# Rotated rows of queries and keys fetched by transfers instead of rotation products

## The reference, cut to what matters

```python
q = apply_partial_rope(rms_norm_2(q.reshape(B, S, 2, DIFF_HEADS, HEAD_DIM), a_q_norm[l]), cos, sin)
k = apply_partial_rope(rms_norm_2(k.reshape(B, S, 2, DIFF_HEADS, HEAD_DIM), a_k_norm[l]), cos, sin)
...
o = diff_attention(q, k, v, lam).transpose(0, 2, 1, 3)
```

## Time and profile before

| | us |
|---|---|
| median of 3 runs | 2271.78 (2271.11 to 2274.24) |
| the profiled execution | 2271.08 |
| its span in the trace | 2269.3 |
| TensorE busy | 2147.4 (95% of the span) |
| VectorE busy | 1237.1 (55%) |
| ScalarE busy | 917.2 (40%) |
| differential stage, from its first to its last instruction | about 1676.6 to 1856 |

### The profile page before, as it was taken

How to read it: one execution, slowest core, us unless ns; L and a number is a source line. 1 busy time by engine, 2 the same in 40 slices (tenths; PEclk the granted TensorE clock), 3 DMA queues, 4 the chain that set the end, 5 groups by cost and what they waited for, 6 DMA issues and landing times. The chain is left out here.

```text
span 2269.3 us, 35754 instructions
## 1 busy us (share of the span) xinstructions
PE 2147.4 (95%) x14668; PEld 1577.5 (70%) x14668; DVE 1237.1 (55%) x2123; ACT 917.2 (40%) x1655; POOL 45.6 (2%) x36
## 2 busy tenths in 40 slices
PE   7999999899999899999989999998999988999998
PEld 5785654588888676766447888886877566887546
DVE  5555443766662375464447666424538774444554
ACT  5424434433332354154344333324346563424462
POOL 2000001000000020000010000000000000000000
PEclk9999999999999999999999999999999999999999
DMA  5201111122223221020112222222321102222001
GB/s 201 75 3 57 57 39 38 67 101 93 93 98 107 75 75 56 22 77 25 50 38 75 93 97 107 93 75 97 114 77 54 38 29 84 93 93 90 23 1 38
DMA packets 23922, 159.82 MB, mean 70 GB/s; under 512 B 3024, under 2 KB 3664, under 8 KB 4944
## 3 DMA queue, kind: packets, MB, share of 16 engines
q1 hardware_dynamic: 23760, 157.53, 19.5%
HBM read 155.43 MB, written 2.10 MB: 69 GB/s over the span
## 5 line engine op out<-in xcount | busy, mean ns | idle before, releaser
L675 DVE TENSOR_TENSOR arena_r<-ring,arena_r 128x512 fp32r<-128x512 f32 x480 | 333.0, 705 | 456.0 <-ACT arena_r L666 453.2
L666 ACT ACTIVATE arena_r<-ring 128x512 fp32r<-128x512 f32 x480 | 296.3, 629 | 601.2 <-PE banks L716 569.1
L714 PE MATMUL banks<-oT_r,arena_r 128*128 128x512 f32 x1136 | 463.0, 408 | 13.4 <-DVE arena_r L675 9.0
L716 PE MATMUL banks<-oT_r,arena_r 128*128 128x512 f32 x1136 | 445.4, 392 | 0.0
L715 PE MATMUL banks<-hT_r,arena_r 128*128 128x512 f32 x1008 | 394.7, 392 | 0.0
L714 PE MATMUL banks<-arena_r,arena_r 128*128 128x512 f32 x688 | 283.2, 412 | 18.0 <-DVE arena_r L706 10.7
L715 PE MATMUL banks<-arena_r,arena_r 128*128 128x512 f32 x720 | 283.2, 393 | 0.0
L716 PE MATMUL banks<-arena_r,arena_r 128*128 128x512 f32 x688 | 270.5, 393 | 0.0
L714 PEld LDWEIGHTS banks<-oT_r,arena_r 128*128 128x128 f32 x1136 | 215.0, 189 | 72.1 <-DVE arena_r L952 10.4
L716 PEld LDWEIGHTS banks<-oT_r,arena_r 128*128 128x128 f32 x1136 | 214.8, 189 | 45.7
L715 PEld LDWEIGHTS banks<-hT_r,arena_r 128*128 128x128 f32 x1008 | 190.5, 189 | 44.8 <-issue 7.9
(11 more groups left out here) (394 smaller groups left out, 2929.8 us busy)
## 6 DMA issues: line engine op xcount, KB each, us to landing
ring<-weights SPq DMA_DIRECT2D x142, 1024.0 KB, 4.8
xT<-x_features SPq DMA_DIRECT2D x2, 1024.0 KB, 6.1
arena<-memory SPq DMA_DIRECT2D x2, 1024.0 KB, 5.1
y_features<-xT SPq DMA_DIRECT2D x8, 256.0 KB, 2.0
const<-constants SPq DMA_DIRECT2D x1, 1088.0 KB, 15.7
const<-constants SPq DMA_DIRECT2D x1, 512.0 KB, 16.4
arena<-positions SPq DMA_DIRECT2D x1, 256.0 KB, 2.7
small<-small_vectors SPq DMA_DIRECT2D x2, 68.5 KB, 6.3
```

The costliest lines, as they stand in the source:

```text
L666: act.activation(hi, self.stream.block(b, n), ACT.Copy).then_inc(self.chip.sem("hi_ready"), 1)
L675: vec.tensor_tensor(lo[:, 0:n * P], self.stream.block(b, n), hi[:, 0:n * P].bitcast(F32), ALU.subtract).then_inc(self.chip.sem("lo_ready"), 1)
L714: pe.matmul(out, w_hi, hi, start=k == 0, stop=False)
L716: ins = pe.matmul(out, w_lo, hi, start=False, stop=k == nk - 1)
```

## The change

The rotation is no longer a product on TensorE. SyncE fetches the rows that are rotated, with transfers from on-chip memory to on-chip memory. Four tiles have 4 x 2 heads x 16 rows = 128 rotated rows, which fill one packed tile (`own`); a second (`other`) gets the same rows with the two halves of 8 swapped. Each tile takes six transfers (per head one of 16 rows of 2 KB into `own` and two of 8 rows into `other`). VectorE then does the three operations once for four tiles instead of once for each, and SyncE writes the 16 rows of each head back, with two transfers for a tile. There are three groups of four tiles: items 3 to 6, 7 to 10 and 11 to 14. VectorE handles them at i = 8, 12 and 15, the last one behind all items. The constant `inv` now has the angles in the packed order and with the sign in them, so that the sine table has the sign; `ropep` is gone. Weight loads keep their conditions but are issued in turn with the new transfers. The first differential unit waits for all 24 transfers back.

```diff
-    put("inv", np.array([inv[(p % 64) % 8] if p % 64 < 16 else 0.0 for p in range(P)])[:, None])
+    put("inv", np.array([-inv[p % 8] if p % 16 < 8 else inv[p % 8] for p in range(P)])[:, None])
...
+ROWS = ((32, 33), (34, 35), (54, 55))
...
-    units[0].needs = (("q_ready", 12), ("dense_used", 6))
+    units[0].needs = (("turned", 12 * 2 * 16), ("dense_used", 6))
...
+    rotated = items[3:]
+    due = {8: 0, 12: 1, n: 2}.get
...
         def _(sp):
-            stream.loads(sp, u0, u1, split)
+            slots = stream.freed(u0, u1)
+
+            def weights(made):
+                while slots and split.last_chunk(slots[0] - RING) < made:
+                    i = slots.pop(0)
+                    sp.wait_ge(chip.sem("lo_ready"), split.last_chunk(i - RING) + 1)
+                    stream.load(sp, i)
+
+            def gather(j):
+                g, at = j // 4, 32 * (j % 4)
+                x, (own, other) = rotated[j][0], (chip.t(i) for i in ROWS[g])
+                sem = chip.sem(f"rows{g}")
+                sp.wait_ge(chip.sem("kn_ready"), j + 4)
+                for e in range(2):
+                    to, of = at + 16 * e, 64 * e
+                    sp.dma_start(own[to:to + 16, :], x[of:of + 16, :]).then_inc(sem, 16)
+                    sp.dma_start(other[to:to + 8, :], x[of + 8:of + 16, :]).then_inc(sem, 16)
+                    sp.dma_start(other[to + 8:to + 16, :], x[of:of + 8, :]).then_inc(sem, 16)
+
+            def put_back(g):
+                sp.wait_ge(chip.sem("q_ready"), g + 1)
+                own = chip.t(ROWS[g][0])
+                for j in range(4 * g, 4 * g + 4):
+                    for e in range(2):
+                        of = 32 * (j % 4) + 16 * e
+                        sp.dma_start(rotated[j][0][64 * e:64 * e + 16, :], own[of:of + 16, :]).then_inc(chip.sem("turned"), 16)
+
+            for i in range(n + 1):
+                if 3 <= i < n:
+                    gather(i - 3)
+                if due(i) is not None:
+                    put_back(due(i))
+                if i < n:
+                    weights(min(v_made[i] // 2 + 4, v_chunks))
+            weights(len(split.chunks))
+            sp.wait_ge(chip.sem("turned"), 12 * 2 * 16)
...
-                if i >= 4:
-                    x, _ = items[i - 1]
-                    pe.wait_ge(chip.sem("kn_ready"), i)
-                    pe.matmul(chip.V.fill(pe), chip.c("ropep"), x, start=True, stop=True).then_inc(chip.sem("v_ready"), 1)
...
+                if due(i) is not None:
+                    own, other = (chip.t(t) for t in ROWS[due(i)])
+                    vec.wait_ge(chip.sem(f"rows{due(i)}"), 4 * 6 * 16)
+                    v(tt(other, other, chip.t(LSIN), ALU.mult))
+                    v(tt(own, own, chip.t(LCOS), ALU.mult))
+                    v(tt(own, own, other, ALU.add), chip.sem("q_ready"))
+                if i < n:
                     split.vector_chunks(vec, v_made[i] // 2 + 4)
-                if i >= 4:
-                    x, _ = items[i - 1]
-                    bank = chip.V.take(vec)
-                    v(tt(TMP, bank, chip.t(LSIN), ALU.mult), chip.sem("v_used"))
-                    v(tt(x, x, chip.t(LCOS), ALU.mult))
-                    v(tt(x, x, TMP, ALU.add), chip.sem("q_ready"))
```

More of the change, by code:

```diff
@@ L197 @@
 for _n, _w in (("ident", P), ("ones", P), ("blk64", P), ("tri", P), ("until", CH),
-               ("strict", CH), ("upper", CH), ("eye", P), ("blk16", CH), ("off32", CH), ("causal", P), ("sbmask", P), ("ropem", P), ("ropep", P),
+               ("strict", CH), ("upper", CH), ("eye", P), ("blk16", CH), ("off32", CH), ("causal", P), ("sbmask", P), ("ropem", P),
                ("levels", 7 * CH), ("decay", 8 * CH), ("hm2", 2), ("hm4", 4), ("eps", 1), ("inv", 1), ("cosm", S), ("sinm", S)):
@@ L251, in constants @@
     put("ropem", r)
[L252 to L257, removed]
     t = np.arange(S)[None, :]
@@ L451 @@
                "f_ready ln_ready kd_ready xl_ready cut_ready silu_ready pt_ready l_ready sum_ready r_ready a_ready  "
-               "rope_ready tab_ready stored mem_ready d_ready").split()
+               "rope_ready tab_ready stored mem_ready d_ready rows0 rows1 rows2 turned").split()
     DELTA_SIGNALS = ("log_ready dcum_ready decay_ready kb_ready nt_ready nf_ready x16_ready inv_ready kt_ready xt_ready  "
@@ L577, in next_loads, with freed @@
             sp.wait_ge(self.chip.w_loaded[b], 16 * (self.loaded + loads + 1))
+    def freed(self, u0, u1):
+        return [i for i in range(RING, self.plan.slots) if u0 <= self.free_after[i] < u1]
     def loads(self, sp, u0, u1, split=None, ahead=0, whole=0):
@@ L2843, in diff_stage @@
     sq, r = [chip.t(work), chip.t(work + 1)], [chip.t(work + 2), chip.t(work + 3)]
-    TMP = chip.t(work + 4)
     sig = chip.t(LSIG)
@@ L2875, in _ @@
             v_walk, g_walk = values(), gates()
[L2876 to L2881, removed]
-                if i >= 4:
-                    x, _ = items[i - 1]
-                    pe.wait_ge(chip.sem("kn_ready"), i)
-                    pe.matmul(chip.V.fill(pe), chip.c("ropep"), x, start=True, stop=True).then_inc(chip.sem("v_ready"), 1)
+            for i in range(n):
+                bank = chip.T.fill(pe)
+                pe.wait_ge(chip.sem("sq_ready"), i + 1)
+                pe.matmul(bank, chip.c("blk64"), sq[i % 2], start=True, stop=True).then_inc(chip.sem("t_ready"), 1)
+                run(v_walk, V_STEPS[i])
             run(g_walk, AHEAD)
-            pe.wait_ge(chip.sem("v_used"), n - 3)
             attn.tensor(pe, Pace(GATE * KD, len(attn.units) + 1, AHEAD, tensor=lambda count: run(g_walk, count)))
```

## The result

| | before | after |
|---|---|---|
| median of 5 runs, us | 2271.78 (2271.11 to 2274.24) | 2285.7 (2284.29 to 2288.8) |
| the profiled execution, us | 2271.08 | 2288.8 |
| its span, us | 2269.3 | 2287.0 |
| TensorE busy, us | 2147.4 | 2143.8 |
| VectorE busy, us | 1237.1 | 1219.2 |

The ratio is 1.0058 (95% interval 1.0047 to 1.007): 13.9 us slower, where 1.9 us faster was forecast. The kernel does what the change says. TensorE and VectorE have less work, as forecast, and the time went the other way.

What follows compares the result with a forecast made beforehand. TensorE was taken as the bound: 10.3 us of products less 0.86, 1.25 and 0.6 for ScalarE leaves 7.6, of which late rows leave 3.6; less 1.7 for the clock gives -1.9, so 2269.9 us, range 2264.0 to 2276.

Steps and rivals of the forecast that it cites:

- the size of one issue: On SP: each small row transfer takes 0.42 us to issue, so 96 take 40.3 us.
- the lower bound: On SP: an issue might cost nothing if its time goes by the number of rows, an eighth or less here.
- the second rival: SP issues cost 0.47 to 0.51 us; gain gone, clock lost, -1 to +4 us, 2270 to 2275; chance 0.14.
- The third rival: SP issues cost 0.52 us or more, backlog also holding VectorE at i = 12; 2278 or 2286 us; chance 0.14.
- the clock: On TensorE at unit 2: after 3.9 us idle, the granted clock drops to about half; 1.7 us lost.
- The distances of sums: On TensorE: sums start 0.86 us closer, items falling to 2.29 us with one value step, 3.73 with two.
- The value steps that wait for ScalarE: After items 4, 9 and 14 TensorE waits for ScalarE to empty value banks, losing 0.86, 1.25 and 0.6 us.
- Landing: Row transfers land 2.0 us after issue, as the stores of 256 KB do.
- does not wait at i = 8: VectorE at the first group: rows there at 1707.5, before the item is normalised at 1708.9, so no wait.
- hardly at i = 12: VectorE at the second group: it hardly waits for rows, 1721.8 against 1722.6.
- it stands 6.6 us: VectorE at the last group: nothing to do from 1729.0 until the rows land at 1735.6.
- The most that the change can give: On TensorE: 10.3 us of removed products less what ScalarE takes back leaves 7.6 us, if nothing else comes last.

Runs made afterwards that it cites:

- e7: The kernel before, with rows of eight unread transfers of each of six forms on SP, to compare the cost of an issue; 2271.78 us (one run).
- e3: The kernel before, products kept, with the change's 96 transfers added on SP into tiles nobody reads; 2272.94 us, ratio 1.0006 to before.
- e1: The changed kernel with the rotation left out altogether: no row transfers, no three operations on VectorE; 2261.87 us, ratio 0.9965 to before.
- e2: The changed kernel with only the gathers of 16 rows, those of 8 rows left out: 48 issues instead of 96; 2262.36 us, ratio 0.996 to before.
- e6: The changed kernel with each tile's second-head transfers issued by GpSimd, 48 there and 48 on SP; 2265.02 us, ratio 0.9972 to before.
- e5: The changed kernel with rows back issued last, VectorE doing group 1 behind all items and group 2 before attention unit 4; 2261.99 us, ratio 0.996 to before.
- e8: The changed kernel with e5 and e6 together: two issue queues, last group before attention unit 4, rows back last; 2266.58 us, ratio 0.9972 to before.
- e4: Like e5, from the changed kernel, but VectorE does group 2 before attention unit 3; 2268.98 us, ratio 0.9993 to before.

## Why the prediction was wrong

**The step that failed** is the size of one issue, "I take 0.42 us: between the 0.38 of a lone one and the 0.49 of a row, since these are rows of six or eight, but small." It is 0.64 in a gather and 0.62 on the way back: 96 issues are 61 us of SP, not 40.3. The rows that bounded it were all transfers with one end in device memory, and the sentence chose among them by size and by place in a row. e7 shows that the kind counts as well: eight in a row take 3.82 us from device memory and 5.02 on the chip, with the same 16 rows of 2 KB. The place in a row counts from device memory (0.35 for the first, 0.48 on the mean), hardly on the chip (0.60 and 0.63). And the lower bound, "nothing, if the time goes by the number of rows", was no bound that anything supported: 8 rows take as long as 128.

The Trainium skill has one figure here ("DMA: Bandwidth & Descriptors", section "Why a DMA increments its semaphore by 16 and not by 1"), the 512 cycles from which the prediction estimated 0.43 us, 0.48 with the gap. The runs have 0.33 to 0.35 for a lone issue from device memory, 0.48 to 0.55 in a row of eight, and 0.54 to 0.68 on the chip: one figure doesn't hold for both kinds. Taken as 0.48 a piece it led to the second rival, 2270 to 2275, nearer than the forecast and still too low.

**The third rival** is what happened, from the point that it gave (0.52 a piece) and with its mechanism: SP's backlog also catches VectorE at the second group, which holds the items behind it. It gave 2286 for 0.65; the median is 2285.7. That it met the median so closely is partly luck: it has slips that cancel, and the profiled stretch lost 15.5 us where the median lost 13.9. 2286 is 14.9 above 2271.1; less the 1.7 for the clock, that leaves the extremes some 13 us later. Against the start of the stretch they are 14.4 later (168.4 and 154.0 us behind it). Unit 2 is only 13.4 later (170.48 and 157.07), since it starts 2.1 us behind the extremes and before started 3.06 behind them; the rival left out this 1 us, which the forecast had counted. The clock then takes 2.1, not 1.7. Windows from unit 2 to unit 8, of after and of before:

```profile
1760.54:1781.02 20.48, 20.48 (x109) 12.90 (x109) 13.78 (x42) 11.89 (x36) 0.00 (x0) 0.85 0.28 85
1744.87:1763.24 18.37, 17.75 (x111) 11.27 (x110) 13.59 (x42) 11.02 (x34) 0.00 (x0) 1.00 0.12 40
```

The third rival was given 0.14, because "all others are under 0.5" was counted as evidence, though none of those others is a transfer of this kind.

**The steps that held**, each by the rows above. The distances of sums: 1710.67 - 1708.38 = 2.29 us with one value step, 1714.40 - 1710.67 = 3.73 with two. The value steps that wait for ScalarE: 0.91 us idle at 1716.33. Item 4's step starts at 1699.42 in after and at 1696.67 in before, 2.75 later, and by this the step at 1716.33 stands at 1713.58, where the prediction has the copies ending at 1713.7. Landing: 1.9 us, 2.0 forecast. The transfers cost almost nothing by themselves, and the weight loads stayed hidden (e3). No wait at unit 8 in after. VectorE "does not wait at i = 8" (1.85 us), waits "hardly at i = 12" (9.0) and "it stands 6.6 us" at the last group (15.9) were wrong; all follow from the one size.

**Terms off in size.** The most that the change can give was put at 7.6 us; e1 has 7.3 at unit 2 and 7.05 at unit 8. The clock was put at 1.7 us; in after it is 2.1 between unit 2 and unit 8, where TensorE is busy all the time. Its 1.4 us before the long wait lie under a wait that comes anyway, and behind unit 8 after is as long as before. That it costs where it falls behind an idle time agrees with the earlier trace rows (0.51 there, 0.50 and 0.57 here).

**The experiments against the theories.** Theory: the time goes by what SP has to issue ahead of the rows that VectorE waits for. e2 (fewer issues), e6 (issues on two queues) and e5 (a later need) each take away one factor of it, and give 20.9, 20.2 and 20.7 of the 22.6 us back; e8, with the last two together, gives 22.3. Rival: the transfers disturb TensorE, VectorE or the weight loads. e3 has all of them, and its unit 8 is only 0.5 us later than before's. Fewer transfers with more rows in each weren't tried.

## What to carry to other kernels

- Price an issue by a row of the same kind, from tile to tile or from device memory. If the trace has none, take the dearest row as the likely value: here a choice 0.2 us too low on 96 issues turned a small gain into 14 us.
- Many small transfers are work of one in-order queue. Lay out their times as for an engine, and ask which engine waits for the last one. If that need can be moved behind other work (e5), their number hardly matters.
- A change that takes work from the bound can lose more than the whole of it: of some 7 us to be had, none was left once 18 us of idle time stood in one place. Keep the wait out of the in-order queue of the engine that feeds the bound.

## What the hardware showed that I had not expected

- SP's issue of a transfer from tile to tile took 0.54 to 0.66 us (three of the 96 in after took 0.71, 0.85 and 1.24), 0.63 to 0.68 a piece in rows of eight, and from device memory 0.33 to 0.35 alone and 0.48 to 0.55 in a row of eight; in rows of eight, the number of rows (8, 16 or 128) and their length (256 bytes or 2 KB) moved it by up to 0.07 us.
- A store from a tile to device memory was issued in 0.33 to 0.35 us, so it is not the source on the chip alone that makes an issue dear.
- GpSimd issued the same transfers in 0.48 to 0.52 us (0.68 for its first), where SP took 0.54 to 0.66 for most, and they landed no later (medians of 1.9 and 2.0 us, SP's 2.4, e6).
- The median landing was 1.9 us for 16 rows of 2 KB (24 transfers back, after), hardly under the 2.0 us of 256 KB.
- After 4.1 us in which TensorE did nothing, although the granted clock in them was 1.00, it had 0.57 in the next 3.9 us (e4).
- The same work behind unit 8 took from 104.45 to 106.17 us in the ten profiled executions, with a mean granted clock of 0.97 or 0.95. A difference of that size in a stretch isn't the change's until its place is found.
